# A two-block network on one core: large SBUF tiles at multiples of 512 bytes, the halves of the weights 128 and 256 bytes past one

## The reference

```python
for l in range(2):                                  # first block
    z = rms_norm(x, norm_mix_w[l]) @ w_in[l] + b_in[l]
    ya = dilated_mixture_attention(q, k, v)         # 8 heads of 64, with partial rope
    yb = sigmoid(o) * norm(mlstm_chunkwise(...))    # 4 heads of 128, after a short conv
    x = x + (ga * (ya @ w_proj_att) + gb * (yb @ w_proj_mlstm)) @ w_out[l]
    x = x + square(relu(rms_norm(x) @ w_ff1[l])) @ w_ff2[l]
x = rms_norm(x, final_norm_w)
...                                                 # second block: an SSD scan, a top-k
...                                                 # attention, a pooling mixer, w_out_2
x = h + (silu(a) * b) @ w_ffn_out_2                 # a, b = split(rms_norm(h) @ w_ffn_in_2)
return rms_norm(x, final_norm_w_2)
```

## Time and profile before

| | us |
|---|---|
| median of 3 runs | 2462.27 |
| the runs | 2462.3, 2460.85, 2462.27 |
| span of the profiled execution, first to last instruction | 2460.9 |
| TensorE busy in it | 2419.6 |
| GpSimd busy | 1109.3 |
| VectorE busy | 1005.7 |
| ScalarE busy | 860.6 |

### The profile page before, as it was taken

How to read it: one execution, slowest core, us unless ns; L and a number is a source line. 1 busy time by engine, 2 the same in 40 slices (tenths; PEclk the granted TensorE clock), 3 DMA queues, 4 the chain that set the end, 5 groups by cost and what they waited for, 6 DMA issues and landing times.

```text
span 2460.9 us, 28776 instructions
## 1 busy us (share of the span) xinstructions
PE 2419.6 (98%) x11108; PEld 1943.8 (79%) x11108; DVE 1005.7 (41%) x1554; ACT 860.6 (35%) x1072; POOL 1109.3 (45%) x808
## 2 busy tenths in 40 slices
PE   8999999999999999999999999999999999999999
PEld 7767888888888767788888887788776688888887
DVE  6646644201203556653310203667594534222202
ACT  4355233421324355333421323441425323322213
POOL 4523354544544523344544544442342354555542
PEclk9999999999999999999999999999999999999999
DMA  4312222222322322223222332321221133232231
GB/s 150 103 56 85 82 86 94 95 103 89 99 103 76 109 69 84 71 86 103 86 103 91 98 103 74 99 78 52 75 86 52 56 103 103 87 101 99 89 103 69
DMA packets 168695, 218.19 MB, mean 89 GB/s; under 512 B 7948, under 2 KB 143052, under 8 KB 168340
## 3 DMA queue, kind: packets, MB, share of 16 engines
q1 hardware_dynamic: 165940, 211.37, 26.6%
q10 hardware_dynamic: 2656, 5.42, 0.6%
HBM read 213.23 MB, written 2.11 MB: 88 GB/s over the span
## 4 chain that ended last, share of the span: by engine, by line
issue 48%; POOL 32%; PE 20%; POOLq 0%; DMA 0%; ACT 0%; DVE 0%; SPq 0%; ACTq 0%
POOL w_lo L284 32%; PE ps L325 4%; PE ps L323 4%; PE ps L324 4%; PE ps L787 3%; PE ps L1834 2%; PE ps L1832 2%; PE ps L1830 2%; POOLq L295 0%; PE ps L2005 0%; PE ps L2672 0%; DMA all_params_norm<-in_norm_mix_w 0%; PE ps L316 0%; PE ps L349 0%; PE ps L343 0%
## 5 line engine op out<-in xcount | busy, mean ns | idle before, releaser
L284 POOL TENSOR_TENSOR w_lo<-w_raw,w_hi 128x512 fp32r<-128x512 f32 x804 | 1109.1, 1412 | 1324.8 <-ACT w_hi L270 1312.2
L270 ACT ACTIVATE w_hi<-w_raw 128x2048 fp32r<-128x2048 f32 x200 | 383.1, 1916 | 1062.0 <-PE ps L325 394.1
L787 PE MATMUL ps<-h_hi,w_hi 128*128 128x512 f32 (+1 forms) x936 | 385.7, 412 | 3.4 <-POOL w_lo L284 3.1
L787 PE MATMUL ps<-h_hi,w_lo 128*128 128x512 f32 (+1 forms) x936 | 366.0, 391 | 0.0
L787 PE MATMUL ps<-h_lo,w_hi 128*128 128x512 f32 (+1 forms) x936 | 365.3, 390 | 0.0
L323 PE MATMUL ps<-h_hi,w_hi 128*128 128x512 f32 x816 | 319.0, 391 | 0.0
L325 PE MATMUL ps<-h_hi,w_lo 128*128 128x512 f32 x816 | 317.5, 389 | 0.0
L324 PE MATMUL ps<-h_lo,w_hi 128*128 128x512 f32 x816 | 317.4, 389 | 0.0
L787 PEld LDWEIGHTS ps<-h_hi,w_hi 128*128 128x128 f32 (+1 forms) x936 | 173.7, 186 | 59.7 <-issue 18.6
L787 PEld LDWEIGHTS ps<-h_hi,w_lo 128*128 128x128 f32 (+1 forms) x936 | 173.3, 185 | 40.7
L787 PEld LDWEIGHTS ps<-h_lo,w_hi 128*128 128x128 f32 (+1 forms) x936 | 173.7, 186 | 40.0 <-issue 4.3
(11 more groups left out here) (410 smaller groups left out, 3544.8 us busy)
## 6 DMA issues: line engine op xcount, KB each, us to landing
w_raw<-in_w_in SPq DMA_DIRECT2D x72, 1024.0 KB, 5.2
w_raw<-in_w_ff SPq DMA_DIRECT2D x64, 1024.0 KB, 5.2
w_raw<-in_w_ffn_in SPq DMA_DIRECT2D x22, 1024.0 KB, 5.0
w_raw<-in_w_out SPq DMA_DIRECT2D x12, 1024.0 KB, 5.0
w_raw<-in_w_ffn_out SPq DMA_DIRECT2D x11, 1024.0 KB, 4.9
w_raw<-in_w_proj_att SPq DMA_DIRECT2D x4, 1024.0 KB, 5.0
w_raw<-in_w_proj_mlstm SPq DMA_DIRECT2D x4, 1024.0 KB, 5.0
w_raw<-in_w_up_ssd SPq DMA_DIRECT2D x4, 1024.0 KB, 5.2
```

Source lines behind the costliest of these rows:

```text
L270: act.activation(k.whi[:, slot * SLOT:(slot + 1) * SLOT], k.wraw[:, slot * SLOT:(slot + 1) * SLOT], ACT.Copy).then_inc(k.hi_done, CHUNKS)
L284: pool.tensor_tensor(k.wlo[:, a:a + T], k.wraw[:, a:a + T], k.whi[:, a:a + T], ALU.subtract)\
L787: mm = pe.matmul(out, lhs, rhs, start=i == 0 and n == 0, stop=stop and n == 2)
```

## The change

Only the starts of tiles change; every instruction, wait and transfer stays. `Kern.top` begins at a multiple of 512 instead of 32, and 128 bytes are left free ahead of w_hi and another 128 ahead of w_lo. All that is placed after them moves up with them, and so does every tile in the arena, whose start follows from `k.top`.

```diff
@@ class Kern, __init__
-        self.top = (nc.sbuf_base + 31) // 32 * 32
+        self.top = (nc.sbuf_base + 511) // 512 * 512
@@ program
         k.hhi, k.hlo = k.keep("h_hi", KD * T, F32R), k.keep("h_lo", KD * T, F32R)
         k.arena, k.arena_words = (k.top + 127) // 128 * 128, ARENA
         k.top = k.arena + 4 * ARENA
-        k.whi, k.wlo = k.keep("w_hi", 2 * SLOT, F32R), k.keep("w_lo", 2 * SLOT, F32R)
+        k.top += 128
+        k.whi = k.keep("w_hi", 2 * SLOT, F32R)
+        k.top += 128
+        k.wlo = k.keep("w_lo", 2 * SLOT, F32R)
         k.xT = k.keep("xT", KD * T)
         k.wraw = k.keep("w_raw", 2 * SLOT)
         k.cst = k.keep("constants", C_END)
```

## The result

The change makes the kernel slower: 2511.41 us (four runs, 2510.06 to 2512.22) against 2462.28 us, a ratio of 1.0198 with a 95% interval of 1.0185 to 1.021, or 49 us. The prediction was 2462 us with a range of 2440 to 2497, and gave "slower" 21%.

What follows compares the result with a forecast made beforehand. TensorE, busy 2419.6 of 2460.9 us, was taken as the bound. Terms: 0 for w_lo, 0 for w_hi, 0 to 2 us elsewhere; with the runs' median 1.4 us above the span, 2462 us, range 2440 to 2497.

Steps and rivals of the forecast that it cites:

- TensorE's stream: About 9,500 float32r matmuls of 128x128 against 512 columns, 226.7 ns apart: 2,154 us of the span.
- The surplus over its columns: Stream's 13.3 ns per matmul above 213.3 ns for 512 columns, 126 us in all, ascribed to SBUF feeding TensorE.
- the price of 0 for a distance of 256: For w_lo, a third of the matmuls, distances 0 and 256 merely change places: 0 us.
- GpSimd's chunks: GpSimd's share of the weight split: median chunk to stay near 1292 ns, effect on the time taken as 0.
- Between them I take 0, for two reasons: w_hi matmuls, about 6,330, moving to distance 128: 0 us chosen between bounds of -84 and +30 us.
- the unit with 8 weight columns: Short weight loads at distances 0 to 224 from h, used as evidence on 128: 231.4 ns per matmul from step 1.
- The first reason: Small unit's starts repeat the same triple from 32 to 224 bytes: a rhythm of short loads, not an address.
- The second: Loads of 8 columns read a sixteenth of the bytes without less surplus, so weight and moving streams hardly collide.
- Rival 2: Unsettled streams: w_hi matmuls lose their lock at distance 128 and stay at 231.4 ns, 2492 us; chance 21%.
- 9,500 matmuls: Estimated count of stream matmuls among TensorE's 11,108 instructions; +45 us if all paid 4.7 ns.
- Its dragged case: Slower rival with the w_lo matmuls between the w_hi ones slowed too: 2507 us, left out of the range.

Runs made afterwards that it cites:

- the four corners: Kernels with and without the two 128-byte pads, each with and without rounding to 512: with pads 2511 us, without 2462, whatever the rounding.
- the map: Separate program of only 33 streams of 72 float32r matmuls, tile starts varied: 226.7 ns per matmul at distance 0, 232.4 with weights at 128.
- the second and third maps: Further stream-only programs: one varied distances, widths, kinds, banks and bfloat16; the other alternated tiles, used 8-column weights and varied what ran ahead. Timed per matmul.

## Why the prediction was wrong

**Right.** TensorE's stream was named as the one large thing that an address could move. The surplus over its columns was put down to the feeding from SBUF; that its size goes by addresses, and that bfloat16 streams show only 2.5 ns of it, fits this without proving it. That only distances matter was right (the four corners), and so was the price of 0 for a distance of 256 (226.7 in the map). GpSimd's chunks stayed as they were, and the waits did not grow. (The waits for w_lo were not 4.0 us before: the list has another 2.4 us at line 342. It changes nothing.)

**Wrong.** The step that failed is "Between them I take 0, for two reasons", the price of distance 128 for w_hi. What was taken as 0 is 6.7 ns per matmul in a settled stream (233.3 for 226.7), paid by the w_lo matmuls too, and 49 us in all. Both reasons leaned on the unit with 8 weight columns, as a probe of distances 32 to 224, and it is no probe. Streams of 8 columns take 231.7 ns at every distance tried from 32 to 224 and 231.1 at 0. Nor were the three matmuls at 226.7 with which that unit begins a sign of what distance 0 gives to short loads: the map's stream of 8 columns at distance 0 starts with 235, 230 and 232 ns and has no such triple. My reading is that the rhythm of the full loads ahead of them ran on for a step; no run tries that by itself. The first reason saw correctly that the pattern is that of short loads, and drew from it that distance is harmless, where it could only mean that this unit says nothing on it. The second, that short loads would have shrunk the surplus if loads and moving tile met, is refuted by full loads that change by 6.7 ns with the distance while short ones stay above 231.

**The rival that came.** Rival 2 had the sign and nearly the size: 2507 us, if the w_lo matmuls were dragged along, and they were. It priced the off pace with the 231.4 ns of the short unit, where the change's stream runs at 233.3, and it took it for a lock that is lost, where the trace shows another lock. That it still came within 5 us is partly luck: 4.7 ns is too little, and charging all 9,500 matmuls with it too much. Its dragged case was left out of the range, and should not have been: in the change's stream and in that with w_lo alone off its place, all three matmuls of a step move to a common rhythm.

Why 6.7 ns and 9,500 matmuls make 49 us and not 63 can be read in the distances. The kernel before did not run at 226.7 ns throughout: with the ten distances of 230 or 231 ns after each interruption its mean is 227.3. The changed one has 233.1, below 233.3 by the wide units above all. These 5.7 ns on some 9,100 distances are 52 us, and the half clock and shorter waits within the stream take off 2 to 3.

**Two rules that the prediction cited.** The Trainium skill, "TensorE: Matmul & The Clock Gate", "Step-by-step: what each phase is for", has two independent read ports for the moving operand and the weights, by which the distance would be worth nothing; for float32r the runs here disagree, by 49 us. The Trainium skill's "Back-to-back issue gap", on the same page, gives 215.8 ns at 512 columns by its formula. The bfloat16 streams meet that exactly, at the three distances tried; no float32r stream of 512 columns came under 226.7. The section calls this the gap of an isolated matmul, though, which the prediction did not say, and has about 131 ns for a sustained stream: no stream of 512 columns here came near that.

**What stays open.** I did not find out what meets in SBUF: both the own and the next weights matter, tiles moved by 16 bytes can change the rhythm or not, and I have no model that gives the curve. The maps have one spacing of slices (512 bytes for the weights, 2,048 for the moving tile); others were not tried. Nor is it shown what the 13.3 ns at the best distance are.

## What to carry to other kernels

Where TensorE streams float32r with 512 columns at full clock, put the stationary and the moving tiles, both halves of each, at the same place modulo 256 bytes; no layout tried is quicker. (At 256 columns distance 128 was quicker by 1.3 ns.) The kernel before had that by luck: its allocator base left nothing to round up at the start of the arena, which stands between h and the weights. A pad "against conflicts" between them can cost 2% with no instruction changed. To judge such a thing from a trace, count starts in a window or take distances from start to start, and don't take a stream of another shape as a witness: a rhythm belongs to the whole stream.

## What the runs showed of the hardware that was not expected

- A float32r stream of 128x128 against 128x512 settles at 226.7 (distance 0) to 234.3 ns (distance 96) per matmul by the distance between its tiles modulo 256, and at distance 128 also by what ran before it (232.4 or 233.3); a bfloat16 stream takes 215.8 at 0, 64 and 128.
- The rhythms are exact: 226.7, 228.9, 230.0, 231.1, 233.3, mostly with patterns of two to seven matmuls that repeat to the nanosecond of the records.
- It matters which matmuls of a step match: with the change's starts, the units whose weights are the moving operand settle at 228.9 ns (one matmul of three matches its own and the next load), the others at 233.3 (none matches both).
- A weight load of 8 columns in place of 128 makes the stream at distance 0 slower, 231.1 for 226.7.
- At the half clock (granted 0.51 in the earlier trace rows) the stream at distance 0 goes at 426.7 ns, the bare columns; the first matmuls of the second and third maps, with w_hi at 128, go at 426 and 427 ns too.
